# Decay and gate projections in 32-row groups of the array, and the logarithms behind the first evictions

## The reference, cut to what matters

```python
z = (u @ w_in).astype(jnp.float32)
gq, gk, gv, gg, ga, mq, mk, mv, mo, mg = jnp.split(z, splits, axis=-1)
a_pre = jnp.einsum('btzr,zre->zbte', ga.reshape(B, T, 2, GLA_RANK), a_up) + a_bias[:, None, None, :]
log_a = (jax.nn.log_sigmoid(a_pre) / GLA_TAU)    # per direction z, 256 channels
mg = (mg.reshape(B, T, 2, 2, MLSTM_HEADS) + ml_gate_bias).transpose(2, 3, 0, 4, 1)
# li = mg[:, 0], lf = log_sigmoid(mg[:, 1]); b = cumsum(log_a within a chunk of 64 tokens)
```

## Time and profile before

| what | value |
|---|---|
| median of 3 runs | 1697.47 us (1695.18 to 1698.81) |
| profiled execution | 1692.29 us, of which the span is 1690.5 us |
| TensorE busy | 1647.2 us, 97% |
| VectorE busy | 1158.8 us, 69% |
| ScalarE busy | 899.5 us, 53% |
| GpSimd busy | 631.5 us, 37% |
| mean granted TensorE clock | 0.991 |
| TensorE on decay inputs (L3463) | 16 records, 63.0 to 79 us |
| TensorE on gate rows (L3483) | 8 records, 83.5 to 86.3 us |

### The profile page before, as it was taken

How to read it: one execution, slowest core, us unless ns; L and a number is a source line. 1 busy time by engine, 2 the same in 40 slices (tenths; PEclk the granted TensorE clock), 3 DMA queues, 4 the chain that set the end, 5 groups by cost and what they waited for, 6 DMA issues and landing times.

```text
span 1690.5 us, 27304 instructions
## 1 busy us (share of the span) xinstructions
PE 1647.2 (97%) x10106; PEld 1456.4 (86%) x10106; DVE 1158.8 (69%) x1808; ACT 899.5 (53%) x1529; POOL 631.5 (37%) x369
## 2 busy tenths in 40 slices
PE   8999999998999999999999999999999999999997
PEld 5777889897899999999888889987668989999886
DVE  4669976667978888888657765245774788886114
ACT  6772435776465555655333453214883547777232
POOL 1132114453234444443443423322005256665444
PEclk8999999999999999999999999999999999999998
DMA  9423224343212233233733333364214122333221
GB/s 360 152 87 125 77 76 145 106 125 137 75 63 76 83 102 93 92 104 103 290 130 117 123 112 126 125 212 156 88 57 150 51 88 101 101 101 106 96 98 63
DMA packets 71239, 197.42 MB, mean 117 GB/s; under 512 B 6322, under 2 KB 27186, under 8 KB 69826
## 3 DMA queue, kind: packets, MB, share of 16 engines
q1 hardware_dynamic: 49268, 177.29, 30.3%
q10 hardware_dynamic: 21840, 18.40, 3.6%
HBM read 187.22 MB, written 8.45 MB: 116 GB/s over the span
## 4 chain that ended last, share of the span: by engine, by line
PE 69%; DVE 18%; ACT 6%; issue 2%; DMA 2%; POOL 1%; DVEq 0%; ACTq 0%; SPq 0%; POOLq 0%
PE ps L3796 18%; PE ps L3999 6%; PE ps L3931 6%; PE ps L3321 6%; PE ps L3425 5%; PE ps L3308 4%; PE ps L3928 3%; PE ps L3307 2%; DMA raw<-in_weights 2%; PE ps L4099 2%; PE ps L3746 2%; PE ps L4078 2%; PE ps L4112 2%; DVE conv L2823 2%; PE ps L3431 1%
## 5 line engine op out<-in xcount | busy, mean ns | idle before, releaser
L889 POOL TENSOR_TENSOR wsp<-raw,wsp 128x1024 fp32r<-128x1024 f32 x110 | 286.6, 2605 | 727.4 <-ACT wsp L1042 726.9
L1042 ACT ACTIVATE wsp<-raw 128x1024 fp32r<-128x1024 f32 x110 | 116.7, 1061 | 173.2 <-PE ps L3308 74.3
L3931 PE MATMUL ps<-hsp,wsp 128*128 128x512 f32 x456 | 154.8, 392 | 0.5 <-DVE hsp L3031 0.5
L3796 PE MATMUL ps<-T,wun 128*128 128x384 f32 (+1 forms) x792 | 148.6, 340 | 4.3 <-DVE ps L2218 2.7
L3796 PEld LDWEIGHTS ps<-T,wun 128*128 128x128 f32 x792 | 141.5, 190 | 5.1 <-issue 4.4
L3321 PE MATMUL ps<-wsp,u 128*128 128x512 f32 x576 | 132.3, 390 | 2.7 <-POOL wsp L889 1.1
L3321 PEld LDWEIGHTS ps<-wsp,u 128*128 128x128 f32 x576 | 107.6, 188 | 27.0 <-issue 2.1
L3308 PE MATMUL ps<-u,wsp 128*128 128x512 f32 (+1 forms) x384 | 125.3, 362 | 0.0
L3425 PE MATMUL ps<-u,wsp 128*128 128x512 f32 x384 | 122.7, 401 | 0.0
L3928 PE MATMUL ps<-hsp,wsp 128*128 128x256 f32 x432 | 119.7, 281 | 1.2 <-DVE hsp L2810 1.2
L3999 PE MATMUL ps<-hsp,wsp 128*128 128x512 f32 x480 | 110.9, 390 | 0.9 <-POOL wsp L889 0.9
(11 more groups left out here) (409 smaller groups left out, 3895.8 us busy)
## 6 DMA issues: line engine op xcount, KB each, us to landing
raw<-in_weights SPq DMA_DIRECT2D x281, 512.0 KB, 3.4
nab<-in_nabias ACTq DMA_DIRECT2D x32, 256.0 KB, 2.7
start_w<-in_start SPq DMA_DIRECT2D x6, 1024.0 KB, 19.9
hidden_scratch<-hid0a SPq DMA_DIRECT2D x16, 384.0 KB, 4.7
hid0a<-hidden_scratch SPq DMA_DIRECT2D x5, 768.0 KB, 6.3
h<-in_x SPq DMA_DIRECT2D x4, 768.0 KB, 7.7
mD<-rows_scratch ACTq DMA_DIRECT2D x12, 256.0 KB, 4.4
mqs<-rows_scratch ACTq DMA_DIRECT2D x12, 256.0 KB, 5.3
```

Source lines behind the costliest of these rows:

```text
L889: pool.tensor_tensor(w[:, 1, :], raw[:, raw_index(s) % 4, :], w[:, 0, :].bitcast(F32), ALU.subtract)\
L1042: act.activation(split_of(s)[:, 0, :], raw[:, raw_s % 4, :], ACT.Copy).then_inc(*own.one(hi_ready))
L3796: mm = pe.matmul(out, UNIT[x][:, wp, tile(i)], operand[:, i, xp, 0:out.shape[-1]], start=(start and i == 0 and a == 0), stop=(i == KH - 1 ...
L3931: mm = pe.matmul(lat_of(layer, g, mm_), w, hsp[:, kk, xp, LAT], start=one, stop=last, skip_group_check=True)
```

## The change

Three orders are changed, and the two kinds of small matmuls.

TensorE: `decay_inputs(zp)`, two matmuls over 128 partitions, four times, becomes `decay_pair(p)`, four matmuls over 32 partitions, twice. A pair does one half p of the channels for both directions; direction z reads partitions 32 z to 32 z + 31 of `small` and `aup` and writes banks 3 + 2 z and 4 + 2 z. The gate rows likewise read the 32 partitions from 64 and from 96 on. The matmuls of the two row groups alternate. One signal stands for a pair, and one for all gate rows. The first pair moves from before the last step of block 2 to after five of the eight steps of projection 3, the second to after two steps of projection 4, and the gate rows to after six.

ScalarE: `evict(2)` comes before the first decay eviction, the evictions of a pair stand together, `evict(3)` stands between them, and `decay_logs((0, 1))` moves from before the last decay eviction to behind `evict(4)`.

VectorE: `turned(3)` moves ahead of `modulate(S_V, 0)`, `turned(4)` ahead of the two running sums.

```diff
--- before.py
+++ after.py
@@ -1306,8 +1306,8 @@
 
             def decay_taken(zp):
 
-                b = 3 + 2 * (zp % 2)
-                act.wait_ge(apre_done.sem, zp + 1)
+                b = 3 + 2 * (zp // 2)
+                act.wait_ge(apre_done.sem, zp % 2 + 1)
                 for t, bank, w in ((LAT, b, N_LAT), (CTX, b + 1, N_CTX)):
                     act.wait_ge(*own.last())
                     act.activation(cum[:, zp, t], ps[:, bank, 0:w], ACT.Identity,
@@ -1321,7 +1321,7 @@
 
             def rows_evict():
 
-                act.wait_ge(rows_done.sem, 2)
+                act.wait_ge(rows_done.sem, 1)
                 for row, b, col in ((rA, 3, 0), (rB, 5, 1)):
                     for t, bank, w in ((LAT, b, N_LAT), (CTX, b + 1, N_CTX)):
                         act.wait_ge(*own.last())
@@ -1386,15 +1386,15 @@
             act.wait_ge(const_loaded.sem, 16 * 5)
             evict(0)
             evict(1)
+            evict(2)
             decay_taken(0)
-            evict(2)
+            decay_taken(2)
+            evict(3)
             decay_taken(1)
-            decay_taken(2)
-            decay_logs((0, 1))
             decay_taken(3)
-            evict(3)
             rows_evict()
             evict(4)
+            decay_logs((0, 1))
 
             def keys_turned(s):
 
@@ -2397,11 +2397,11 @@
             turned(2)
             modulate(3, 0)
             modulate(4, 0)
+            turned(3)
             modulate(S_V, 0)
+            turned(4)
             running_sum(0)
             running_sum(1)
-            turned(3)
-            turned(4)
 
             def step():
                 dve.wait_ge(*own.last())
@@ -3452,37 +3452,38 @@
                 if ks[-1] == KT - 1:
                     mm.then_inc(*own.one(block_used))
 
-            def decay_inputs(zp):
-                b = 3 + 2 * (zp % 2)
-                if zp >= 2:
-                    pe.wait_ge(apre_taken.sem, 2 * (zp - 1))
-                elif zp == 1:
+            def decay_pair(p):
+
+                if p == 0:
                     pe.wait_ge(in_act_took.sem, 3)
                     pe.wait_ge(in_dve_took.sem, 2)
-                for t, bank, w in ((LAT, b, N_LAT), (CTX, b + 1, N_CTX)):
-                    mm = pe.matmul(ps[:, bank, 0:w], aup[:, zp // 2, tile(zp % 2)], small[:, t], start=True, stop=True)
+                else:
+                    pe.wait_ge(apre_taken.sem, 4)
+                for x, (t, w) in enumerate(((LAT, N_LAT), (CTX, N_CTX))):
+                    for z in range(2):
+                        rows = slice(32 * z, 32 * z + 32)
+                        mm = pe.matmul(ps[:, 3 + 2 * z + x, 0:w], aup[rows, z, tile(p)], small[rows, t], start=True, stop=True)
                 mm.then_inc(*own.one(apre_done))
 
             for b in range(2):
                 first_row(b, 6)
                 first_row(b, 7)
             first_row(2, 6)
+            first_row(2, 7)
+            projection(3, range(5))
             pe.wait_ge(const_loaded.sem, 16 * 5)
-            pe.wait_ge(in_act_took.sem, 1)
-            decay_inputs(0)
-            first_row(2, 7)
-            projection(3, range(4))
-            decay_inputs(1)
-            decay_inputs(2)
-            projection(3, range(4, KT))
-            decay_inputs(3)
-            projection(4, range(4))
+            decay_pair(0)
+            projection(3, range(5, KT))
+            projection(4, range(2))
+            decay_pair(1)
+            projection(4, range(2, 6))
             pe.wait_ge(apre_taken.sem, 8)
-            for c, b in ((0, 3), (1, 5)):
-                for t, bank, w in ((LAT, b, N_LAT), (CTX, b + 1, N_CTX)):
-                    mm = pe.matmul(ps[0:64, bank, 0:w], sel[:, c, :], small[:, t], start=True, stop=True)
-                mm.then_inc(*own.one(rows_done))
-            projection(4, range(4, KT))
+            for x, (t, w) in enumerate(((LAT, N_LAT), (CTX, N_CTX))):
+                for c in range(2):
+                    rows = slice(64 + 32 * c, 96 + 32 * c)
+                    mm = pe.matmul(ps[0:64, 3 + 2 * c + x, 0:w], sel[rows, c, :], small[rows, t], start=True, stop=True)
+            mm.then_inc(*own.one(rows_done))
+            projection(4, range(6, KT))
 
             def gla_turned(s):
```

## The result

| | before | after |
|---|---|---|
| median of 6 runs | 1697.88 us (1695.18 to 1700.81) | 1705.32 us (1704.03 to 1707.29) |
| ratio, 95% interval | | 1.0048 [1.0037, 1.0059] |
| profiled execution | 1692.29 us, span 1690.5 | 1705.25 us, span 1703.5 |

A forecast was written before the change was run, and what follows sets the result against it. TensorE, busy 97%, bounds the kernel, decided here by block 7's 1.2 us margin. Block 7 later, +4.8, and clock, +1.6, sum to +6.4 us: 1692.29 becomes 1698.7, the median 1703.9, range 1699.3 to 1708.6.

The forecast's parts named there:

- Pairs: TensorE's small matmuls: a pair of row groups, and the gate rows, each take 1.45 us, between ends of 1.33 and 2.87.
- Rival 1: TensorE's 32-row groups don't run beside each other, steps take 2.87 us: +10.7, 1708.2 us; chance 0.12.
- rule of the drain: Changing TensorE's tiling mode drains the array: estimated 0.14 us a change, six add 0.8, making +7.2 instead of +6.4.
- TensorE's gain: On TensorE from block 3 to the value blocks, 4.35 us of pairs and gate rows replace the old steps and gaps: -3.5 us.
- term of 1.1 for gaps: Gaps and pipeline fill left over in TensorE's 24.6 us before the value blocks, 1.1 us, counted as going away.
- ScalarE's chain: First logarithms at 91.75, second at 101.25, block 7's low part at 112.9 instead of 108.1: TensorE idles 8.4 us, +4.8.
- Nothing takes it back: After block 7 on TensorE, blocks 7 and 8 run without waits and release what follows, so the delay stays.
- rival 2: The delay is taken back later, or the clock's lower level falls elsewhere: +1, 1698.5 us; chance 0.12.
- Clock: TensorE's idle time is followed by its 1.2 GHz level: +1.6 us, between ends of 0 and 3.2.
- Rival 3: TensorE's gain stays because block 7's low part is ready by 104.5: -3.5 us, 1693.9 us; chance 0.10.
- VectorE's and SyncE's queues: The product with weight tile 6 and two loads stand behind the running sums, product 5 about 1 us later: taken as nothing.

The follow-up runs named there:

- e6: The kernel before with only its small matmuls cut to the 32 partitions that hold weights, in their old order; 1.0002 of the kernel before.
- e1: The changed kernel with ScalarE making block 7's high part ahead of the logarithms of (2,3); 0.9984 of the kernel before, 1695.15 us.
- e8: The changed kernel unaltered, measured again; 1.0043 of the kernel before, 1705.99 against 1697.97 us.
- e2: The changed kernel with 17 otherwise useless matmuls filling TensorE's wait between value blocks 6 and 7; 1.0023 of the kernel before.
- e4: The kernel before with only the moved logarithms and VectorE's new order, TensorE unchanged; 1.0043 of the kernel before.
- e3: The changed kernel with an own buffer for the fourth pair's logarithm, so logarithms (2,3) skip the wait for the running sum; 1.0026 of the kernel before.
- e7: The changed kernel with both block 7's high part ahead of logarithms (2,3) and the fourth logarithm's own buffer; 0.9979 of the kernel before, 1693.06 us.

## Why the prediction was right

Direction, place and mechanism came as forecast. Step by step:

- *Pairs:* 1.45 forecast, 1.49 measured to the next matmul, 1.44 for the gate rows. Rival 1 is out. But the forecast set 1.45 against 2.67 and 1.33, which count the late first pass behind a step too; with its 0.12 a pair costs 1.61. That is 0.28 above the 1.33 of full pairing, and it isn't that the groups pair badly: in e6 a step of one direction takes 1.48 and one of both 1.49, so the second direction is free, and the 0.28 comes with the 32-row step itself, even where one row group works alone. By the Trainium skill's rule of the drain on changing the tiling mode ("TensorEngine Tiling (Array Packing)", Tiling Modes, Key Properties) the sum would have been 7.2. The prediction's estimate for that rule was 0.14 for one change, so 0.28 for the two of a step, which agrees in size with the trace; no run here separates a drain from fill.
- *TensorE's gain:* -3.5 forecast; block 3 to block 5 took 24.6 before and 21.86 after, -2.7. About half of the missing 0.8 is the pairs and gate rows (1.61 twice and 1.55 instead of 1.45). Most of the rest is the term of 1.1 for gaps: the first 15 passes took 5.46, 0.364 each and not the 0.346 read later in the stretch, so 0.3 of what I had called gaps was pass time and stayed.
- *ScalarE's chain:* first logarithms 91.75 forecast, 91.70 measured; second 101.25 and 101.15; block 7 on TensorE 112.9 and 112.75, with 7.99 of wait where 8.4 was forecast. That these times agree to 0.15 is partly luck: this execution's block 3 started 0.43 earlier, and what was lost on TensorE made up for it. Counted from block 3's start, block 7 is 5.1 later than before; 4.8 was forecast.
- *Nothing takes it back:* block 9 starts 7.6 later after block 3, the time is 7.4 longer. So rival 2 is out. The two profiled executions differ by 13.0, since the rest of the program, behind block 9's start, took 1565.6 in the one of before and 1571.5 in that of after; in those of e1 to e8 it lies between 1567 and 1575, whatever the change. So the sum, added to the median, is held against medians.
- *Clock:* +1.6 forecast from the earlier trace rows, +2.5 in the trace (18.98 for 72 records at 0.2287 each) and 2.3 by e2. The mechanism held and the size was too small: the lower level lasted 5.0 us into the work, where in the earlier trace rows it was over within 3.4. The length of the wait doesn't give this: 2.9 us in e4 and 6.2 in e3, after waits of 8.05 and 6.75 (last section). This term (0.9) and block 7's start (0.3) make up the difference between 6.4 and the 7.6 at block 9.
- *Rival 3* said what it would take: block 7's low part before TensorE asks. e1 supplies just that, by another way than the one weighed (ScalarE far ahead), and the gain comes: e1 and e7 lie 2.7 and 3.6 us below the kernel before, near the 3.6 of that rival.
- *VectorE's and SyncE's queues* were taken at nothing: product 6 ran at 104.08, as worked out, and no wait of TensorE between blocks 3 and 9 ends on a load.

## What to carry to other kernels

A group of operations that is taken out of a place where its engine ran ahead isn't free at its new place: look for the next thing on the same engine that the bounding engine will ask for, and compare the two times; here 1.2 us of margin met 9.5 us of work. When a wait appears, first try to exchange the two neighbours on the engine that is late (e1), before giving up the change. A gain on the busiest engine shows only once the engines that feed it keep up (e6 against e1).

## What the runs showed of the hardware

- Two row groups of 32 partitions ran beside each other whether their matmuls alternated (the changed kernel, 1.49 us for four) or came one direction after the other (e6, 1.49). In e6 the second direction's matmul of 512 columns overtook the first's of 256, which stands ahead of it in the program: the four records of 512 columns start from 69.73 to 70.27, those of 256 from 70.66 on.

```profile
69.73 1.13 PE L3463 MATMUL ps<-small,aup 32*128 32x512 f32 x4 [0.38 <-DVE gqk L2376]
```

```profile
70.66 0.63 PE L3463 MATMUL ps<-small,aup 32*128 32x256 f32 x4
```

- A step of two 32-row matmuls by itself isn't shorter than one over 128 partitions but longer: 1.48 us to the next matmul and 0.11 for the late first pass (e6, from 62.12), against 1.10 and 0.19 (before, from 62.99 and from 73.16).
- How long TensorE's granted clock stayed at 1.2 GHz after work went on varied: 5.0 us in the changed kernel after a wait of 7.99, 6.2 in e3 after 6.75, 2.9 in e4 after 8.05. Blocks 7 and 8 lost half of that each time: 2.5, 3.0 and 1.5 us. The stretches of e3 and e4, columns as above:

```profile
110.60:116.80 6.20, 6.20 (x15) 4.86 (x16) 6.06 (x5) 1.99 (x5) 2.97 (x1) 0.50 0.25 85
114.94:117.80 2.86, 2.86 (x7) 2.28 (x8) 2.83 (x2) 2.77 (x6) 2.84 (x1) 0.50 0.54 183
```
